# Order of the last expert pair's weight loads, and token stores by halves from two queues

## The reference, cut to what matters

```python
def hier_moe(h, wg, bg, we, be, w1, w3, w2):
    x = h.reshape(-1, D)
    ...                       # comb: (tokens, 16), two non-zero weights a token
    h1 = jnp.einsum('nd,edf->nef', x, w1)      # w1, w3: 16 x 1024 x 512
    h3 = jnp.einsum('nd,edf->nef', x, w3)
    a = jax.nn.silu(h1) * h3 * comb[:, :, None]
    return jnp.einsum('nef,efd->nd', a, w2)    # w2: 16 x 512 x 1024

for l in range(DEPTH):
    ...                       # mixer, xp = xp + gate * op
    xp = xp + mp[5] * hier_moe(hp, ...)
    xs = xs + ms[5] * hier_moe(hs, ...)
return (xp, xs, new_cache_k, new_cache_v)
```

## Time and profile before

| | |
|---|---|
| median of 3 timed runs | 815.8 us (814.9 to 817.2) |
| the profiled execution's own time | 817.36 us |
| its span, first to last instruction | 815.5 us |
| mean granted TensorE clock | 0.994 of full speed |
| PE, DVE, ACT busy | 778.3, 335.8, 176.7 us |
| bytes moved by DMA | 277.44 MB |

### The profile page before, as it was taken

The page is one execution under the profiler, slowest core; times in us unless marked ns, Lnnn a source line. Parts: engine busy times, 40 slices in busy tenths (PEclk is TensorE's granted clock), DMA queues, the critical chain, the costliest instruction groups (busy, mean ns, idle before and its releaser), DMA issues.

```text
span 815.5 us, 10146 instructions
## 1 busy us (share of the span) xinstructions
PE 778.3 (95%) x3987; PEld 382.2 (47%) x3987; DVE 335.8 (41%) x750; ACT 176.7 (22%) x420; POOL 2.2 (0%) x9
## 2 busy tenths in 40 slices
PE   7899999999899999999978999999899999999986
PEld 3364545545444444444325657545444444444333
DVE  2216088225822644345307202225822644345316
ACT  3111566205411101110113401105411101110111
POOL 0000000000000000000000000000000000000000
PEclk9999999999999999999999999999999999999999
DMA  9979999924499999999999962024499999999993
GB/s 366 415 269 429 379 403 426 386 103 154 156 386 421 421 422 421 421 422 420 422 420 426 428 269 104 0 104 158 153 384 421 420 420 422 422 421 420 421 420 132
DMA packets 40050, 277.44 MB, mean 340 GB/s; under 512 B 8589, under 2 KB 9505, under 8 KB 11073
## 3 DMA queue, kind: packets, MB, share of 16 engines
q1 hardware_dynamic: 39649, 275.28, 82.4%
q10 hardware_dynamic: 288, 1.34, 0.4%
q0 software_dynamic: 64, 0.13, 0.0%
HBM read 275.04 MB, written 1.70 MB: 339 GB/s over the span
## 4 chain that ended last, share of the span: by engine, by line
PE 84%; DMA 7%; DVE 4%; ACT 2%; issue 1%; DVEq 1%; ACTq 0%; SPq 0%
PE bank L1881 24%; PE bank L1898 13%; PE bank L1779 10%; DMA ring<-in_moe_w 6%; PE bank L1866 6%; PE bank L1904 5%; PE bank L2273 4%; PE bank L1717 4%; PE bank L2136 4%; PE bank L2098 3%; PE bank L2294 1%; PE bank L2188 1%; PE bank L1759 1%; PE bank L1730 1%; PE bank L2209 1%
## 5 line engine op out<-in xcount | busy, mean ns | idle before, releaser
L1881 PE MATMUL bank<-ring,Z 128*64 128x512 f32 x1024 | 226.2, 594 | 8.4 <-DMA ring<-in_moe_w 5.6
L1881 PEld LDWEIGHTS bank<-ring,Z 128*64 128x64 f32 x1024 | 73.5, 137 | 145.8 <-issue 144.0
L1898 PE MATMUL bank<-ring,Z 128*64 128x512 f32 (+1 forms) x544 | 113.9, 570 | 0.7 <-DMA ring<-in_moe_w 0.7
L1779 PE MATMUL bank<-ring,T 128*128 128x512 f32 x192 | 83.1, 593 | 1.2 <-ACT T L1136 1.2
L1898 PEld LDWEIGHTS bank<-ring,Z 128*64 128x64 f32 x544 | 38.0, 137 | 68.5 <-issue 66.8
L1406 DVE TENSOR_TENSOR Z<-Z,bank 128x512 f32<-128x512 f32 x16 | 11.0, 688 | 134.9 <-PE bank L1881 134.9
L1779 PEld LDWEIGHTS bank<-ring,T 128*128 128x128 f32 x192 | 36.2, 190 | 45.6 <-issue 45.6
L1904 PE MATMUL bank<-ys,Cs 128*128 128x512 f32 (+1 forms) x204 | 52.3, 391 | 1.1 <-DVE ys L1423 1.1
L1436 DVE TENSOR_TENSOR x<-x,bank 128x512 f32<-128x512 f32 x84 | 52.0, 681 | 0.3
L1083 ACT ACTIVATE ys<-wg 128x512 fp32r<-128x512 f32 (+1 forms) x34 | 20.6, 605 | 136.1 <-DVE wg L1418 136.1
L1400 DVE COPY Z<-bank 128x512 f32<-128x512 f32 x24 | 16.6, 692 | 78.8 <-PE bank L1866 78.8
(11 more groups left out here) (237 smaller groups left out, 746.3 us busy)
## 6 DMA issues: line engine op xcount, KB each, us to landing
ring<-in_moe_w SPq DMA_DIRECT2D x192, 1024.0 KB, 15.8
ring<-in_ada_w SPq DMA_DIRECT2D x23, 2048.0 KB, 14.6
ring<-in_a_w_out SPq DMA_DIRECT2D x2, 2048.0 KB, 12.0
ring<-in_f_w_in SPq DMA_DIRECT2D x2, 2048.0 KB, 28.7
ring<-in_f_w_out SPq DMA_DIRECT2D x2, 2048.0 KB, 27.8
ring<-in_ada_w SPq DMA_DIRECT2D x2, 1024.0 KB, 8.4
ring<-in_a_w_in SPq DMA_DIRECT2D x4, 512.0 KB, 19.4
ring<-in_a_w_in SPq DMA_DIRECT2D x1, 2048.0 KB, 32.5
```

Source lines behind the costliest of these rows:

```text
L1779: last = pe.matmul(b[:, :], T[:, k, i * P:(i + 1) * P], w[:, k, :], start=(k == 0), stop=(k == KT - 1))
L1881: last = pe.matmul(out[BLK * u:BLK * (u + 1), :], xT[:, b, k, s0 + BLK * u:s0 + BLK * (u + 1)], w[:, k, :], start=(k == 0), stop=(k == KT ...
L1898: last = pe.matmul(end_banks[n][BLK * u:BLK * (u + 1), 0:e - a], aT[:, k, BLK * u:BLK * (u + 1)], w2[:, FC * hh + k, a - HALF * hh:e - HAL ...
```

## The change

Three things are changed.

1. The last pair's loads. The halves of w1 are issued in turn of both experts: first halves of u = 0 and u = 1, then the second halves. For w3 and w2 the first halves of both are issued, then the third quarters of both, then the last quarters of both. The last quarters of w3 and w2 have semaphores of their own (arrived_end), and TensorE waits for them only before the matmuls that use them: the last two blocks in w3, and columns 768:1024 in w2.
2. For that, w2's columns lie in the order of END_PARTS on a partition: 4 blocks of 512, 4 of 256, 4 of 256. A last quarter of w2 is so a contiguous run of 4 KB on each partition. In all other pairs the right half of the down product (512 columns) reads two runs of 256 in one matmul.
3. The stores of the tokens. Each block is stored in two halves of the columns. The left half waits for the additions of columns 0:512, the right half for those of 768:1024, both by VectorE's count of additions (back_out). SP stores the left halves and the right halves of blocks 0 and 2, ACT the right half of block 1. In layer 1 VectorE no longer drains and counts x_ready behind the last additions.

```diff
+        arrived_end = [sem(f"arrived_end{i}") for i in range(4)]
...
+        def store_tokens(e, i, a, b, backs):
+            e.wait_ge(pairs[L - 1]["back_out"], (NPAIR - 1) * 2 * NT + backs)
+            dst = y_prompt[0] if i == 0 else y_sample[0, (i - 1) * P:i * P, :]
+            e.dma_start(dst[:, a:b], x[:, i, a:b]).then_inc(out_done, 16)
...
+                def expert_words(e, k, w, half, a, b, landed=None):
+                    n = n0 + k
+                    sp.wait_ge(*last_use(n - NS, half))
+                    if landed is None:
+                        landed = (arrived, arrived_late)[half][n % NS]
+                    sp.dma_start(ring[:, n % NS, a:b], w[l, e, :, a:b]).then_inc(landed, 16)
...
                 p = NPAIR - 1
-                for k, (u, w) in enumerate(items):
-                    expert(2 * p + u, 6 * p + k, w)
+                cuts = [0, SLOT // 2, 3 * SLOT // 4, SLOT]
+                for half in range(2):
+                    for u in range(2):
+                        expert_words(2 * p + u, 6 * p + u, moe_w1, half, SLOT // 2 * half, SLOT // 2 * (half + 1))
+                for m in (2, 4):
+                    for c in range(3):
+                        for u in range(2):
+                            expert_words(2 * p + u, 6 * p + m + u, items[m][1], min(c, 1), cuts[c], cuts[c + 1],
+                                         arrived_end[m - 2 + u] if c == 2 else None)
...
             for i in range(NT):
-                sp.wait_ge(x_ready, 3 * NT + i + 1)
-                dst = y_prompt[0] if i == 0 else y_sample[0, (i - 1) * P:i * P, :]
-                sp.dma_start(dst, x[:, i, :]).then_inc(out_done, 16)
-            sp.wait_ge(out_done, 16 * NT)
+                store_tokens(sp, i, 0, HALF, i + 1)
+            for i in (0, 2):
+                store_tokens(sp, i, HALF, D, 2 * NT + i + 1)
+            sp.wait_ge(out_done, 16 * 2 * NT)
...
+            store_tokens(act, 1, HALF, D, 2 * NT + 2)
...
                     last_back(2, i)
-                    settle()
-                    dve.sem_inc(x_ready, 1)
-                    if l == 0 and i > 0:
-                        norm(2, i - 1)
+                    if l == 0:
+                        settle()
+                        dve.sem_inc(x_ready, 1)
+                        if i > 0:
+                            norm(2, i - 1)
...
+                def down_columns(w2, k, a, e):
+                    if (a, e) == (HALF, D):
+                        return w2[:, FC * a:FC * e].rearrange("p (c k n) -> p c k n", c=2, k=FC)[:, :, k, :]
+                    return w2[:, FC * a:FC * e].rearrange("p (k n) -> p k n", k=FC)[:, k, :]
...
+                    def arrive_end(k):
+                        for u in range(2):
+                            pe.wait_ge(arrived_end[k - 2 + u], 16 * (l + 1))
...
                         up_part(out, q % 2, s0, weights(k), 0, KT // 2).then_inc(s["up_half"], 1)
+                        if last and k == 2:
+                            arrive(k, 1)
+                            up_part(out, q % 2, s0, weights(k), KT // 2, KT - 2)
+                            arrive_end(k)
+                            up_part(out, q % 2, s0, weights(k), KT - 2, KT).then_inc(s["up_full"], 1)
+                            return
...
                     for k in range(FC):
                         if k == FC // 2:
                             last_backs(0)
+                        if k == 0:
+                            arrive_end(4)
                         done = down(k, 2, ws, *END_PARTS[2])
...
-    for name, widths in (("moe_w1", [DE]), ("moe_w3", [DE]), ("moe_w2", [HALF, HALF])):
+    for name, widths in (("moe_w1", [DE]), ("moe_w3", [DE]), ("moe_w2", [e - a for a, e in END_PARTS])):
```

More of the change, by code:

```diff
@@ L837, in _ @@
                         weights(N_MIX1 + n, src)
-                def expert(e, k, w):
[L840 to L844, removed]
+                def expert_words(e, k, w, half, a, b, landed=None):
[4 more added lines that the diff above has]
+                    sp.dma_start(ring[:, n % NS, a:b], w[l, e, :, a:b]).then_inc(landed, 16)
+                def expert(e, k, w):
+                    for half in range(2):
+                        expert_words(e, k, w, half, SLOT // 2 * half, SLOT // 2 * (half + 1))
                 items = [(0, moe_w1), (1, moe_w1), (0, moe_w3), (1, moe_w3), (0, moe_w2), (1, moe_w2)]
@@ L1893, in combine_rows @@
                     last.then_inc(s["comb_full"], 1)
+                def down_columns(w2, k, a, e):
+                    if (a, e) == (HALF, D):
+                        return w2[:, FC * a:FC * e].rearrange("p (c k n) -> p c k n", c=2, k=FC)[:, :, k, :]
+                    return w2[:, FC * a:FC * e].rearrange("p (k n) -> p k n", k=FC)[:, k, :]
                 def down(k, n, ws, a, e):
-                    hh = a // HALF
                     for u, w2 in enumerate(ws):
-                        last = pe.matmul(end_banks[n][BLK * u:BLK * (u + 1), 0:e - a], aT[:, k, BLK * u:BLK * (u + 1)],
-                                         w2[:, FC * hh + k, a - HALF * hh:e - HALF * hh], start=(k == 0), stop=(k == FC - 1), skip_group_check=True)
+                        out = end_banks[n][BLK * u:BLK * (u + 1), 0:e - a]
+                        if (a, e) == (HALF, D):
+                            out = out.rearrange("p (c n) -> p c n", c=2)
+                        last = pe.matmul(out, aT[:, k, BLK * u:BLK * (u + 1)],
+                                         down_columns(w2, k, a, e), start=(k == 0), stop=(k == FC - 1), skip_group_check=True)
                     return last
@@ L1924, in arrive, with slots @@
                                 pe.wait_ge(arrived[n % NS], 16 * (n // NS + 1))
+                    def arrive_end(k):
+                        for u in range(2):
+                            pe.wait_ge(arrived_end[k - 2 + u], 16 * (l + 1))
+                    def slots(k):
+                        return [ring[:, n % NS, :] for n in (n0 + 6 * p + k, n0 + 6 * p + k + 1)]
                     def weights(k):
-                        return [ring[:, n % NS, :].rearrange("p (k n) -> p k n", k=KT)
-                                for n in (n0 + 6 * p + k, n0 + 6 * p + k + 1)]
+                        return [w.rearrange("p (k n) -> p k n", k=KT) for w in slots(k)]
                     def up(out, k):
@@ L1983, in pair @@
                     pe.wait_ge(s["act_cols"], p + 1)
-                    ws = weights(4)
+                    ws = slots(4)
                     def last_backs(n):
@@ L2044, in moe @@
                             pe.wait_ge(o["weights"], j * 48 + 48)
-                            ow = [ring[:, m, :].rearrange("p (k n) -> p k n", k=KT) for m in range(3)]
+                            ow = [ring[:, m, :].rearrange("p (k n) -> p k n", k=KT) for m in range(2)]
                             up_part(psA, 0, 0, ow[0:1], 0, KT).then_inc(o["up_full"], 1)
@@ L2054, in moe @@
                                 for k in range(FC):
-                                    done = down(k, hh, ow[2:], HALF * hh, HALF * (hh + 1))
+                                    done = down(k, hh, [ring[:, 2, :]], HALF * hh, HALF * (hh + 1))
                                 done.then_inc(o["down_full"], 1)
```

## The result

The changed kernel took 809.13 us (median of 4 runs, 808.28 to 811.23) beside 816.44 us (4 runs, 814.9 to 817.2) of the kernel before: ratio 0.9907, 95% interval 0.989 to 0.9924. Twice more, each time beside 17 runs of the kernel before, the ratio was 0.9935 (0.9914 to 0.9956) and 0.9900 (0.9871 to 0.9929). In microseconds the medians lie 7.3, 6.6 and 7.9 apart. The forecast was a gain of 6.4 us, to 809.4.

The account below looks back on a forecast made before the run. The weight stream was taken to bound each layer's last pair. Layer 0's 2.3, layer 1's 2.2 and the stores' 1.9 sum to 6.4 us: 815.8 to 809.4 us, range 806.8 to 811.6, reaching to 812.8 for 8 in 10.

Parts of the forecast that it names:

- The bound and the landing times by position: Last pair of each layer: the weight stream bounds; each queue position keeps its landing time, 2.5 us per 1 MB piece.
- Layer 0: Last pair of layer 0: w3 starts sooner, behind position 6 instead of 7; gain 2.3 us (2.15 to 2.45).
- The "issue" gap: Before layer 0's last pair, 2.8 us: if it stays the gain there is 2.15 us, if a weight wait 2.45.
- Layer 1: Last pair of layer 1: w2 starts 2.5 us sooner, less 0.3 us for the quarters; gain 2.2 us.
- The price of the quarters: Last pairs' half-MB loads: 0 to 0.11 us more per quarter; 0.3 us taken in layer 1, hidden in layer 0.
- SP's order: SP's load queue: issues wait longer for free slots, but some 10 pieces in flight hide it; cost nothing.
- The operand of two runs: Right-half down products of 14 other pairs, 224 matmuls reading two runs of 256: cost taken as 0, at most 2.0 us.
- The stores: End of the kernel: token stores by halves and additions without drains end it 1.9 us sooner (1.0 to 2.5).
- (a): Last pairs: waits go in one layer alone, or late quarters make new 1 us waits; gain 4.2 us, 811.6; chance 0.12.
- (b): Last pairs: the end of w2 decides, so no waits are won, only the stores; 813.9 us; chance 0.07.
- (c): Quarters of w3 and w2: each pays a fixed 1.4 us; slower, 830 us; chance 0.05 together with the two-run operand rival.
- (d): Two-run operand costs over 0.033 us in each of 224 matmuls; slower, 831 at 0.1; chance 0.05 with the fixed-price rival.

Follow-up runs that it names:

- all quarters: Changed kernel with w1, w3 and w2 of the last pair all in quarters of 512 KB, each with its own wait: 812.3 us, ratio 0.9912.
- no branch: Changed kernel without TensorE's skipped block for experts with more than 64 tokens, run twice: 809.0 and 808.9 us, ratios 0.9886 and 0.9887.
- columns only: Kernel before with only w2's columns in the new order, loads and stores as before: 817.0 us, ratio 0.9988.
- order only: Changed kernel with the stores as before: new order of the last pair's weights, quarters and w2 columns kept; 810.5 us, ratio 0.9918.
- fine pieces: Changed kernel with w3 and w2 of the last pair in pieces of 256 KB: 813.2 us, ratio 0.9932.
- no quarters: Changed kernel with w3's and w2's second halves as whole 1 MB pieces, in turn of both experts: 812.7 us, ratio 0.9937.
- stores only: Kernel before with the changed kernel's stores by halves from two queues, old order of weights kept: 816.7 us, ratio 0.9986.
- quarters without turn: Changed kernel with quarters and their signals, but all pieces of expert u = 0 before those of u = 1: 815.5 us, ratio 0.9976.
- stores from one queue: Changed kernel with all six store halves issued by SP, none by ACT: 809.9 us, ratio 0.9895.

## Why the prediction was right

The mechanism held in both layers and in the stores, term by term. That the median came within 0.3 us of the forecast is luck: medians of this kernel are uncertain by 1 to 2 us, the kernel before stood at 816.4 and not 815.8 beside it, and the three comparisons gave 6.6 to 7.9 us.

**The bound and the landing times by position.** Two loads of layer 1's last pair, positions 6 and 10 (issue plus time to landing), land at 757.3 + 22.5 = 779.8 and 768.6 + 22.3 = 790.9. By the kernel before, shifted by the 4.81 us of the stretch's start, they were to be at 779.6 and 790.8. w3 starts at 779.95, w2 at 791.06.

```profile
L852 SPq DMA_DIRECT2D ring<-in_moe_w x1: 328/328/328, 757.3 to 757.3; - x1
...
DMA to landing us min/median/max: 22.5/22.5/22.5
...
L852 SPq DMA_DIRECT2D ring<-in_moe_w x1: 2136/2136/2136, 768.6 to 768.6; - x1
...
DMA to landing us min/median/max: 22.3/22.3/22.3
```

**Layer 0**, 2.3 us: measured 2.42. The "issue" gap was left open as of unknown cause, with both outcomes priced; it stayed, since it belongs to the branch. The weights of the next stage, put at nothing, cost nothing: the 0.69 us by which the way to layer 1's last pair differs go with the clock.

**Layer 1**, 2.2 us: measured 2.33, from w2's start. The margin before the last quarter held: there is no gap in the down product. TensorE's waits for weights fell to 1.9 us, just under the 2 to 4 foretold.

**The price of the quarters**, 0 to 0.11 us each with 0.3 us taken in layer 1: by the rate of the kernel with all quarters 0.03 each, so some 0.13 us at w2's first halves. Even that can't be seen there: from position 6 to position 10 it takes 11.1 us in the changed kernel and 11.2 in that of before, both with a step that is told of under no branch. The stores from which I took the upper bound go at 387 GB/s; the same 4 KB rows as loads go at 410. This is the size that was off, by 0.2 to 0.3 us.

**SP's order** at nothing: right in its effect. An issue now takes up to 3.7 us, since the queue is full, and its landing stays in its place.

**The operand of two runs** at nothing: right, shown by columns only.

**The stores**, 1.9 us: measured 0.45 + 1.5 = 1.95; the additions stand 0.33 us apart without the drains, and the last store lands 2.7 us at most after its issue. The span ends 3.1 us behind the last addition, a little over the 2.7 to 3.0 foretold. The range's lower end, by its own sum (808.3 less 1.4), is 806.9 and not 806.8.

**The rivals.** (a), the gain in one layer alone, and (b), nothing but the stores, are refuted by A and B of order only. (c), a fixed price for each piece, by fine pieces. (d) by columns only. The Trainium skill's rule of at least 1 MiB per DMA ("DMA: Bandwidth & Descriptors", section "Bandwidth") held here in its direction only: pieces of 0.5 MB and 256 KB slow a full stream by 2% and 8%, where its fit for DMAs issued by GpSimd (section "Anatomy of one DMA") has about 2 us of fixed time for each.

**What the prediction did not see** is the clock behind the gaps, below, which moved the comparison of single executions by 1.7 us and more, though not the medians beyond the range; and that the landing times it took as fixed hold a step of about 1 us in each layer's last pair that goes with the branch (no branch, above).

## What to carry to other kernels

When a product takes pieces of two tensors and the load stream is the bound, order the pieces by when they are first needed, and only then cut them finer: here the turn alone gave 1.6 us, finer signals alone nothing, both 4.8. Cut only the pieces whose wait ends last; beyond that, here, each piece cost and nothing was left to win. Look too at what else the DMA engines move beside the stream: here a packet of the instruction queue went with the one late piece of each last pair. Where a median can't tell one part of a change, distances between fixed instructions in the profile can, once the stretches at a lower clock are told apart.

## What was not expected of the hardware

**TensorE's clock falls behind some gaps of 2.2 to 2.8 us, and not behind others as long.** In layer 0 TensorE stands for 2.5 to 2.8 us before the last pair in eleven profiles with the branch, and for 2.24 in a twelfth (no quarters). In five of the twelve the product behind it took 8.4 to 10.1 us in place of 7.1, at a granted clock of 0.50, that is the lower of its two levels (1.2 GHz); in layer 1, behind a gap of 2.4 us for w3, in one of four (stores only). In layer 0 it fell in neither of two profiles with a gap of 2.4 or 2.5 us for w3 (columns only, quarters without turn). Behind the shorter waits of 0.2 to 2.1 us in the last pairs it fell in none. But further on, near 445 us, TensorE stands for 2.2 us in all 14 profiles, and there the clock fell in eight. So neither the length of the gap nor the kernel tells whether it falls, and the cause is open. The stretches of the second profile of the changed kernel and, below, of stores from one queue:

```profile
411.50:413.50 2.00, 2.00 (x8) 0.73 (x6) 0.00 (x0) 0.00 (x0) 0.00 (x0) 0.50 1.01 406
413.50:415.50 2.00, 2.00 (x12) 0.74 (x10) 0.00 (x0) 0.00 (x0) 0.00 (x0) 0.86 1.00 403
```
```profile
412.10 10.09 PE L1900 MATMUL bank<-ring,Z 128*64 128x512 f32 x32 [2.79 <-issue]
```

What it costs depends on what comes next. In stores only, a fall of 1.7 us in layer 0 was paid out of the wait for w3, which shrank from 2.1 to 0.4 us; A did not change. In the changed kernel that wait is gone, and the same fall makes A 1.5 us longer. So a part of the gain in layer 0 is given back in the executions where the clock falls, while in layer 1 the change takes away the gap behind which it could. Which of the two is larger over many executions is open.

**A full queue holds the issuer, not the data.** SP's issue of a load takes 0.33 us, and up to 3.7 us when ten loads of 1 MB and 0.5 MB are in flight. The load of w2's first half of u = 0 in layer 1 took 3.7 us to issue and landed 2.5 us behind the piece before it, as its bytes ask.
